# Condition products on VectorE, copied state rows, 64x64 retention tiles and wide statistics in a four-layer kernel

## The reference

```python
# hybrid layers: two condition vectors c, c_ctx (1024 each) give shift, scale, gate
c_act = silu(c); cc_act = silu(c_ctx)
shift, scale, gate = split(c_act @ w_mod[l] + b_mod[l], 3)        # w_mod: (2, 1024, 3072)
mod_c = split(cc_act @ w_mod[l][:, :n_mod * 1024] + b_mod[l][...], n_mod)
# S5: states (complex, 64 per group) and outputs per group of 16 channels
y = einsum('bsgp,gcp->bsgc', states, C).real + d_skip * u
# retention, chunks of 128, heads of 64
scores = einsum('bhnid,bhnjd->bhnij', qc, kc) * dmat
# dilated attention: the three groups are weighed by their log-sum-exp
wts = softmax(stack(lses), axis=0)
```

## Time and profile before

| what | us |
|---|---|
| median of 3 runs (3162.23 to 3170.07) | 3165.14 |
| the profiled execution | 3164.52 |
| its span, first to last instruction | 3162.7 |
| PE busy | 3082.5 (97%) |
| DVE busy | 1413.5 (45%) |
| ACT busy | 1224.7 (39%) |
| POOL busy | 805.0 (25%) |

### The profile page before, as it was taken

The page is one execution under the profiler, slowest core; times in us unless marked ns, Lnnn a source line. Parts: engine busy times, 40 slices in busy tenths (PEclk is TensorE's granted clock), DMA queues, the critical chain, the costliest instruction groups (busy, mean ns, idle before and its releaser), DMA issues.

```text
span 3162.7 us, 48297 instructions
## 1 busy us (share of the span) xinstructions
PE 3082.5 (97%) x19259; PEld 2501.3 (79%) x19259; DVE 1413.5 (45%) x3281; ACT 1224.7 (39%) x2582; POOL 805.0 (25%) x407
## 2 busy tenths in 40 slices
PE   7999999999999998999999999999999999999999
PEld 6877778788777887777887888877788778877777
DVE  3342131221213125659432635564546845564566
ACT  4443434444343434512221523355433433354342
POOL 2155554111111114133255111111123111111231
PEclk9999999999999999999999999999999999999999
DMA  6113223144423333423453421111103322111113
GB/s 198 45 49 87 79 68 87 53 129 118 115 76 111 94 89 102 137 70 100 140 186 114 139 54 41 32 34 25 30 28 114 114 79 54 33 34 32 36 47 140
DMA packets 327767, 261.83 MB, mean 83 GB/s; under 512 B 78123, under 2 KB 291659, under 8 KB 327548
## 3 DMA queue, kind: packets, MB, share of 16 engines
q1 hardware_dynamic: 187692, 131.09, 14.4%
q10 hardware_dynamic: 139856, 127.69, 13.6%
HBM read 215.50 MB, written 45.97 MB: 83 GB/s over the span
## 4 chain that ended last, share of the span: by engine, by line
PE 52%; DVE 4%; ACT 2%; issue 2%; DMA 1%; POOL 0%; ACTq 0%; DVEq 0%; SPq 0%; POOLq 0%
PE psum L1534 26%; PE psum L387 9%; PE psum L312 5%; PE psum L1646 2%; PE psum L1666 2%; PE psum L1655 2%; PE psum L3161 1%; PE psum L1571 1%; DVE act_lo L2558 1%; PE psum L1561 1%; PE psum L3152 1%; PE psum L1577 1%; PE psum L3136 0%; PE psum L1604 0%; DVE arena L2320 0%
## 5 line engine op out<-in xcount | busy, mean ns | idle before, releaser
L2742 POOL TENSOR_TENSOR w_lo<-w_raw,w_hi 128x1024 fp32r<-128x1024 f32 x122 | 300.1, 2460 | 1450.6 <-ACT w_hi L3242 758.0
L1534 PE MATMUL psum<-act_hi,w_hi 128*128 128x512 f32 (+1 forms) x1376 | 512.6, 373 | 9.5 <-ACT arena L1759 5.2
L2912 PE MATMUL psum<-act_hi,w_hi 128*128 128x512 f32 x1280 | 505.5, 395 | 6.3 <-ACT arena L1211 5.4
L2912 PE MATMUL psum<-act_lo,w_hi 128*128 128x512 f32 x1280 | 507.5, 396 | 0.0
L2912 PE MATMUL psum<-act_hi,w_lo 128*128 128x512 f32 x1280 | 504.1, 394 | 0.0
L1534 PE MATMUL psum<-act_lo,w_hi 128*128 128x512 f32 (+1 forms) x1376 | 503.9, 366 | 0.0
L1534 PE MATMUL psum<-act_hi,w_lo 128*128 128x512 f32 (+1 forms) x1376 | 503.6, 366 | 0.0
L1534 PEld LDWEIGHTS psum<-act_hi,w_hi 128*128 128x128 f32 x1376 | 260.0, 189 | 63.1 <-issue 15.0
L3719 DVE CUSTOM_DVE_ANT_0 arena<-psum,arena 128x256 f32<-128x256 f32 (+2 forms) x384 | 103.6, 326 | 456.9 <-PE psum L2961 179.9
L1534 PEld LDWEIGHTS psum<-act_hi,w_lo 128*128 128x128 f32 x1376 | 259.9, 189 | 45.2 <-issue 5.1
L1534 PEld LDWEIGHTS psum<-act_lo,w_hi 128*128 128x128 f32 x1376 | 260.2, 189 | 43.0 <-issue 5.8
(11 more groups left out here) (402 smaller groups left out, 5258.1 us busy)
## 6 DMA issues: line engine op xcount, KB each, us to landing
w_raw<-in_attn_w_in SPq DMA_DIRECT2D x80, 512.0 KB, 3.7
w_raw<-in_w_in SPq DMA_DIRECT2D x64, 512.0 KB, 4.0
spare<-in_w_mod ACTq DMA_DIRECT2D x24, 1024.0 KB, 8.2
x<-arena ACTq DMA_DIRECT2D x24, 512.0 KB, 2.9
arena<-weight_rows ACTq DMA_DIRECT2D x16, 512.0 KB, 6.7
w_raw<-in_ssm_w_in SPq DMA_DIRECT2D x16, 512.0 KB, 3.6
arena<-mc_mat ACTq DMA_DIRECT2D x16, 512.0 KB, 3.6
arena<-x ACTq DMA_DIRECT2D x16, 512.0 KB, 5.4
```

The costliest lines, as they stand in the source:

```text
L1534: ins = nc.tensor.matmul(psum[:, n % 2, 0:c], w[:, slot % 2, k * P:(k + 1) * P], a[:, k, c0:c0 + c], start=(m == 0), stop=(m == 23))
L2742: G.tensor_tensor(w_lo[:, par], w_raw[:, par], w_hi[:, par].bitcast(F32), ALU.subtract).then_inc(slot_split, 1)
L2912: ins = nc.tensor.matmul(psum[:, h % 2, :], w[:, (3 + j) % 2, k * P:(k + 1) * P], a[:, k, c:c + 512], start=(m == 0), stop=(m == 23))
```

## The change

Four edits.

1. *Condition products.* DVE now does the multiplications. `mod_part(dve, n, quarter)` runs at i = 4, 5, 6, 7 of the segment before the block's own, 8 instructions each, 32 for a block: for each of 8 depths k and 2 conditions a 128x256 multiply (k = 0) or multiply-and-add into `MOD_SUM`. Each waits for the last but one before it. `mod_mul` is 8 matmuls with a stationary side of ones that add up the partitions; they now stand ahead of `outputs` of step 1 and use that step's bank. `mod_add` moves there too. The weights' loads are issued at i = 0 and must land before i = 4; they wait for DVE's last part instead of PE.
2. *Copied states.* 16 copies of 128x512 bring the states of two groups into contiguous rows: 8 on ACT for half 0 between `load_mc` and `take_z(1)`, 8 on DVE for half 1 behind the scan. PE waits for each by itself.
3. *Retention.* The inner scores are four matmuls of 64 rows x 64 columns, one for each quarter of the array.
4. *Statistics.* Their transpose takes 128 columns (`STAT_WIDE`, zero beyond the 32 in use) and writes 128 rows.

```diff
+        def pack_states(copy, half, i):
+            return copy(packed_rows(half, i).rearrange("p (a r) t -> p a r t", a=2),
+                        ST[half][:, 0:P, :, 2 * i:2 * i + 2].rearrange("p t r a -> p a r t"))
...
-        def mod_mul(pe, n):
-            pe.wait_ge(m_wide, 2)
-            pe.wait_ge(m_w, 32 * (n + 1))
-            for k in range(KT):
+        def mod_part(dve, n, quarter):
+            half, k0 = quarter // 2, KT // 2 * (quarter % 2)
+            dve.wait_ge(m_w, 32 * (n + 1))
...
+            if n > 0:
+                dve.wait_ge(m_mul, n)
+            done = 32 * n + 16 * half
+            for k in range(k0, k0 + KT // 2):
+                for i in range(2):
+                    w, total = MOD_W[half][:, k, :], MOD_SUM[:, i, CTX * half:CTX * half + CTX]
+                    c = c_cols[:, k, i:i + 1]
+                    if k == 0:
+                        nc.vector.tensor_scalar(total, w, c, None, ALU.mult).then_inc(m_part, 1)
+                    else:
+                        dve.wait_ge(m_part, done + 2 * k + i - 1)
+                        nc.vector.scalar_tensor_tensor(total, w, c, total, ALU.mult, ALU.add).then_inc(m_part, 1)
+        def mod_mul(pe, n, bank):
...
+            pe.wait_ge(m_part, 32 * (n + 1))
+            if n > 0:
+                pe.wait_ge(m_sum, n)
+            for i in range(2):
                 for c in range(4):
-                    ins = nc.tensor.matmul(psum[32 * c:32 * c + 32, 6, 0:P], c_wide[:, k, :],
-                                           MOD_W[c // 2][:, k, P * (c % 2):P * (c % 2) + P],
-                                           start=(k == 0), stop=(k == KT - 1))
+                    ins = nc.tensor.matmul(psum[32 * c:32 * c + 32, bank, 384:512], MOD_ONE[:, i, :],
+                                           MOD_SUM[:, i, P * c:P * c + P], start=(i == 0), stop=(i == 1))
...
-                    for h in range(2):
-                        ins = nc.tensor.matmul(psum[:, inner_banks(n)[h], 0:P], tk[HALF[h], n * P:(n + 1) * P],
-                                               tq[HALF[h], n * P:(n + 1) * P], start=True, stop=True)
+                    for e in range(2):
+                        for h in range(2):
+                            half = h ^ e
+                            ins = nc.tensor.matmul(psum[HALF[half], inner_banks(n)[h], 0:P],
+                                                   tk[HALF[h], n * P + 64 * half:n * P + 64 * half + 64],
+                                                   tq[HALF[h], n * P:(n + 1) * P], start=True, stop=True, skip_group_check=True)
...
-                if p % 4 == 0 and mod_of(hp, si) is not None:
-                    pe.wait_ge(m_sum, mod_of(hp, si) + 1)
+                if p % 4 == 1 and mod_of(hp, si) is not None:
+                    mod_mul(pe, mod_of(hp, si), OB(p))
...
-                    ins = nc.tensor.transpose(psum[0:4 * NT, OB(p), 2 * P:3 * P],
-                                              STAT[:, (3 * hp + si) % 2].rearrange("p a b -> p (a b)"), ident[:, :])
+                    ins = nc.tensor.transpose(psum[:, OB(p), 2 * P:3 * P], STAT_WIDE[:, (3 * hp + si) % 2], ident[:, :])
...
-                if mod_of(hp, si) is not None:
-                    if si == 1:
-                        proj(hp, h0, at, at + 8)
-                        at += 8
-                    pe.wait_ge(u_evac, NU * hp + (8 if si == 1 else 8 * si - 2))
-                    mod_mul(pe, mod_of(hp, si))
...
+                if half == 0:
+                    pe.wait_ge(s_out, 2 * NP + i + 1)
+                else:
+                    pe.wait_ge(q_dve, Q_OPS + i + 1)
...
-                            nc.tensor.matmul(psum[:, b0 + g2, a * P:(a + 1) * P], ST[half][r, 0:P, ri, 2 * i + a],
+                            nc.tensor.matmul(psum[:, b0 + g2, a * P:(a + 1) * P], packed_rows(half, i)[r, 2 * a + ri],
...
-                    if i == 5 and -1 <= m < N_MOD - 1:
+                    if i == 0 and -1 <= m < N_MOD - 1:
                         if m >= 0:
-                            act.wait_ge(m_mul, m + 1)
+                            act.wait_ge(m_part, 32 * (m + 1))
                         load_mod_w(act, m + 1)
...
+                if p % 4 == 1 and mod_of(hp, p // 4) is not None:
+                    mod_add(dve, mod_of(hp, p // 4), OB(p))
...
+                    n = 3 * (hp - 4) + si + 1
+                    if i >= 4 and 0 <= n < N_MOD:
+                        mod_part(dve, n, i - 4)
```

More of the change, by code:

```diff
@@ L817, in state_rows, with packed_rows @@
             return ST[h][:, 1:129].rearrange("p j r g -> p g r j")[:, 2 * n:2 * n + 2]
+        def packed_rows(half, i):
+            if half == 1:
+                return region(8192 + 512 * i, 4, P)
+            if i == 7:
+                return YR[:, 6, 512:1024].rearrange("p (q c) -> p q c", q=4)
+            c = P * ((i + 1) // 2)
+            return YR[:, 4 * (i % 2):4 * (i % 2) + 4, c:c + P]
+        def pack_states(copy, half, i):
+            return copy(packed_rows(half, i).rearrange("p (a r) t -> p a r t", a=2),
+                        ST[half][:, 0:P, :, 2 * i:2 * i + 2].rearrange("p t r a -> p a r t"))
         def state_cols(n):
@@ L1223, in build @@
         mod_rows = dram("mod_rows", (2, 2, 3072))
-        m_wide, m_c, m_mul, m_sum, m_stored = [sem(n) for n in ("m_wide", "m_c", "m_mul", "m_sum", "m_stored")]
+        m_part, m_c, m_mul, m_sum, m_stored = [sem(n) for n in ("m_part", "m_c", "m_mul", "m_sum", "m_stored")]
         m_bias, m_w = sem("m_bias"), sem("m_w")
@@ L1245, in load_mod_bias, with mod_add @@
                               ).then_inc(m_bias, 16)
-        def mod_mul(pe, n):
-            pe.wait_ge(m_wide, 2)
-            pe.wait_ge(m_w, 32 * (n + 1))
-            for k in range(KT):
+        def mod_part(dve, n, quarter):
+            half, k0 = quarter // 2, KT // 2 * (quarter % 2)
+            dve.wait_ge(m_w, 32 * (n + 1))
+            if n == 0 and quarter == 0:
+                dve.wait_ge(m_c, 33)
+                dve.wait_ge(k_put, CHUNK_PUT * N_CHUNKS)
+            if n > 0:
[11 more added lines that the diff above has]
+        def mod_mul(pe, n, bank):
+            if n == 0:
+                pe.wait_ge(n_pad, 3)
+            pe.wait_ge(m_part, 32 * (n + 1))
+            if n > 0:
+                pe.wait_ge(m_sum, n)
+            for i in range(2):
                 for c in range(4):
-                    ins = nc.tensor.matmul(psum[32 * c:32 * c + 32, 6, 0:P], c_wide[:, k, :],
-                                           MOD_W[c // 2][:, k, P * (c % 2):P * (c % 2) + P],
-                                           start=(k == 0), stop=(k == KT - 1))
+                    ins = nc.tensor.matmul(psum[32 * c:32 * c + 32, bank, 384:512], MOD_ONE[:, i, :],
+                                           MOD_SUM[:, i, P * c:P * c + P], start=(i == 0), stop=(i == 1))
             ins.then_inc(m_mul, 1)
-        def mod_add(dve, n):
+        def mod_add(dve, n, bank):
             if n == 0:
@@ L1262, in mod_add @@
             dve.wait_ge(m_mul, n + 1)
-            nc.vector.tensor_tensor(MOD_ROWS[:, n], MOD_ROWS[:, n], psum[:, 6, 0:P], ALU.add).then_inc(m_sum, 1)
+            nc.vector.tensor_tensor(MOD_ROWS[:, n], MOD_ROWS[:, n], psum[:, bank, 384:512], ALU.add).then_inc(m_sum, 1)
         def store_mod(act, l):
@@ L3558, in _ @@
                 load_mc(i)
+            act.wait_ge(q_dve, Q_OPS // 2 + 4)
+            for i in range(NP):
+                pack_states(nc.scalar.copy, 0, i).then_inc(s_out, 1)
             take_z(1)
@@ L3938, in _ @@
             assert n_q[0] == Q_OPS, n_q[0]
+            dve.wait_ge(s_out, 3 * NP)
+            for i in range(NP):
+                pack_states(V.tensor_copy, 1, i).then_inc(q_dve, 1)
             stage_mark(dve)
```

21 lines of the change are left out of this document (10 added, 11 removed).

## The result

The changed kernel takes 3193.97 us (median, 3190.43 to 3195.75) against 3166.9 of the kernel before on the same chip: a ratio of 1.0086 with a 95% interval of 1.0071 to 1.0101. It is 27 us slower. The forecast was 3169 with a range up to 3187: the time lies outside it, on the side of the first rival.

The account below looks back on a forecast made before the run. PE, busy 97% of the span, was taken as the bound, along with whatever makes it wait. Terms -15.4 + 25.8 + 1 + 5.1 - 10.9 - 2.7 + 1 = +3.9 us on 3165.1 gave 3169 us, range 3149 to 3187.

Parts of the forecast that it names:

- the first rival: DVE's inserted work ahead of the copy of step 2 costs more, 0.42 us an instruction: 3185 us, chance 0.26.
- part 2: Condition products on DVE, 11 us a block: mostly in idle time, but stalling PE at segment 0's copy of step 2.
- 1. PE's part: Condition products on PE: a block falls from 1.88 to 0.6 us, saving 15.4 us over 12 blocks.
- 2. DVE's part: Condition products on DVE: 32 instructions a block at 0.345 us each, ends 0.285 and 0.42.
- The replay at the copy: Segment 0, head pairs 4 to 7: sixteen instructions and POOL's lock delay the copy of step 2, +25.8 us together.
- The second sixteen: A block's other DVE instructions, behind segment 0's copy and ahead of segment 1's logits: +1 us in all.
- 3. The clock: Low granted clock after the stalls at the copy, 1.7 us for each of three new ones: +5.1 us.
- 4. Copied states: `carried` calls fall from 1.96 to 1.28 us through contiguous weight loads, 16 calls: -10.9 us; the copies are hidden.
- the rival from the rule on columns: Weight load time depends on columns alone, so the state copies bring nothing: 3180 us, chance 0.04.
- 5. Retention: Inner scores in four quarters: 0.64 to 0.54 us for two chunks, 27 pairs, -2.7 us.
- 6. Statistics: 24 transposes with 128 stationary columns instead of 32: +1 us, range -1 to +2.
- The costlier stalls: Stalls at the copy grow with 0.42 us instructions and second stretches of low clock: 3185 us, chance 0.26.

Follow-up runs that it names:

- four_sums: The changed kernel with four running sums taken in turn instead of two, so each instruction waits for the fourth last: 3190.47 us, ratio 1.0076.
- copy_first: The changed kernel with all 32 DVE instructions of a block in segment 0 placed behind the copy of step 2: 3201.09 us, ratio 1.0107.

## Why the prediction was wrong, point by point

**What bounds the kernel** was read rightly: PE's busy time fell by 15 us and the time rose, by waits and by the low clock behind them. But the view stopped at the place where the kernel before already waited. The step that failed is the sentence of part 2, "In segments 1 and 2 DVE has nothing behind the logits of the last step but short copies, and PE doesn't need it before `proj` is through". It was priced at nothing, and so was the whole queue behind it ("`proj` covers PE until then"). It holds for head pairs 4 to 6. In head pair 7 segment 2 has no `proj`, and POOL's row of eight operations stands there: a wait of 19.7 us where the kernel before had 1.4. That one place cost 18.5 of the 31 us between the two traces. The loads, priced at nothing there too, did hold: DVE never stood idle for them.

**1. PE's part.** 1.28 us a block forecast. In segment 2 of head pairs 4, 5 and 6, where no wait is new, the stretch is 1.43 us shorter although the wider statistics cost 0.045 in it: 1.47 a block, 17.7 instead of 15.4.

**2. DVE's part.** The instruction was taken at 0.345 us and is 0.396, above the value of 0.37 from which the first rival was to decide. The reason that I gave for the lower value (each waits for the last but one only) was right and beside the point: `four_sums` shows that the wait plays no part. The bound of 0.42 was nearer. Dividing the kernel's own two-source operation, 1.14 us for 1024 columns, by four gives 0.285; if the two are alike, 0.396 for 256 columns says that some 0.15 us of each doesn't shrink with the columns (an estimate from these two figures).

The replay at the copy gave +25.8 and +21.7 was measured. Its DVE part fits, by two errors that nearly cancel: at head pair 4 from the merge's start to the copy 705.35 - 694.41 = 10.94 us against 5.15 + 5.5. The sixteen took 6.06 for 5.5, the merge 4.88 for 5.15. POOL's share was wrong in half of the places: I let DVE lose the port each time, and at 4 and 5 POOL lost it. In the Trainium skill ("SBUF — State Buffer", "SBUF: two separate sides") whichever operation starts first keeps the shared ports until it is over and the other is blocked. The blocking is what the rows show. That the first to start is the next to go is not: at 699.69 POOL was ahead of nine DVE instructions that started later, and all of them went first.

The second sixteen were priced at +1. PE's waits for ScalarE (L2953) grew by 8.8 - 5.4 = 3.4 us in all; in `copy_first` the same wait grows to 42.9, so it is the same shortage of idle time.

**3. The clock.** The size was off. In the windows behind the four restarts (columns as in the earlier trace rows) PE ran at its level of 1.2 GHz nearly throughout:

```profile
705.00:711.00 6.00, 5.02 (x35) 3.85 (x36) 6.00 (x13) 0.59 (x1) 2.71 (x1) 0.50 0.30 90
860.00:866.00 6.00, 5.40 (x37) 4.15 (x38) 6.00 (x13) 0.59 (x1) 2.33 (x1) 0.54 0.31 88
1016.00:1022.00 6.00, 5.08 (x35) 3.92 (x36) 6.00 (x18) 0.58 (x1) 0.00 (x0) 0.50 0.08 24
1167.00:1173.00 6.00, 5.19 (x36) 4.00 (x37) 6.00 (x17) 0.58 (x1) 0.00 (x0) 0.53 0.07 20
```

20.7 us of work at half speed are about 10.3 lost, 1.7 of them there before: +8.6 where I had +5.1. I had charged a stall of 7 us with what one of 4.5 had cost.

These terms for the eleven blocks, -16.2 + 21.7 + 3.4 + 8.6 + 0.5 for the statistics, make +18.0 of the +21.3 in the table; one more stretch of low clock behind a wait at 873 us is 1.7 of what is left, and the rest I can't place.

**4. Copied states.** The mechanism held and the rival from the rule on columns fell: a weight load takes 188 ns in place of 310 for the same 128 columns, so the Trainium skill ("TensorE: Matmul & The Clock Gate", LDWEIGHTS), which counts columns alone, does not cover a strided source; the measurement decides. The gain per call was under-sized (0.87 us for 0.68, 13.9 in all for 10.9). What I had not asked is what a faster consumer runs into: the ring's loads were priced nowhere, and took back 3 us and the clock behind them. -7.8 us remained in this trace, -8 to -13 in the others.

**5. Retention**: -2.7 forecast, -4.6 measured; a record takes 0.030 us, not 0.034. **6. Statistics**: +1 forecast, 24 x 0.045 = +1.1 measured.

**Left open.** +6.5 us lie between head pair 7 and the S5 outputs. Some are low clock behind short waits; the largest (PE for DVE at the residual, 0.4 us before, 2.0 after) shows 0.4 to 2.4 us over the fourteen traces without following any edit. It was not studied, nor were 2 us of the last stretch that the retention does not explain.

**The rivals.** The costlier stalls came nearest, in spacing and in time (3185). But their price did not come where they had it: the four stalls at the copy grew by 21.7 us, less than the forecast's 25.8, so that the nearness in time is luck. None had the mechanism that decided. The range was built from the spread of known places, and a place left out is not in such a range.

## What to carry to other kernels

When work moves to an idle engine, look at every place where it lands, and first at the ends of a loop, where the cover of the next round is missing; one odd pass out of twelve cost 18.5 us here, more than PE saved in all twelve. Read the idle gaps in the trace of before and put the work into gaps longer than it is, away from rows of GpSimd operations: the same 384 instructions cost 40 us in one placing and gained about 18 in another (3149.70 to 3131.84, with their loads and matmuls moved along). And when a consumer gets faster, check its loads next, with every other queue that loads at that time.

## What the runs showed of the hardware

- DVE and POOL exclude one another where both read SBUF, and the effect goes both ways: a DVE instruction of 0.475 us took 2.1 to 2.6, and a POOL operation of 2.4 us took 8.02 and 9.51 while DVE went on with nine or more. With both queues full they alternated one to one, which made 5.6 us of DVE work 20.5.
- A 128x256 `scalar_tensor_tensor` from SBUF starts every 0.396 us, the same with two running sums and with four.
- Matmuls of 64 rows with 128 moving columns: 0.122 us a record with a strided stationary side, 0.068 with a contiguous one, 0.030 in four quarters of the array.
- One extra load of 512 KB beside a ring of three that takes 512 KB every 2.18 us came with a wait of PE of 0.4 to 3.5 us in ten traces; in the one run with that load moved to a later place among the calls the wait moved with it, and behind the ring's last load it was 0.2.
